# Mixture of experts in fixed slots: ranked groups, weights kept for two blocks, and a half block with stacked parts

## The reference, cut to what matters

```python
g_sel = jnp.argmax(g_logits, axis=-1)                      # one of 4 groups for each token
e_logits = jnp.take_along_axis(e_logits, g_sel[:, None, None], axis=1)[:, 0]
top_p, top_i = lax.top_k(e_prob, 2)                        # two of its 4 experts
combine = jnp.sum(one_hot(g_sel[:, None] * 4 + top_i, 16) * (g_w * top_p)[..., None], axis=1)
hid = silu(einsum('nd,edf->nef', hf, w_gate)) * einsum('nd,edf->nef', hf, w_up)   # f = 256
hid = hid * combine[..., None]
out = einsum('nef,efd->nd', hid, w_down)
```

## Time and profile before

| | |
|---|---|
| median of 3 runs | 1088.68 us |
| profiled execution: span | 1090.1 us |
| TensorE, matmul | 1073.4 us busy, 98% of the span |
| VectorE | 726.9 us, 67% |
| ScalarE | 617.3 us, 57% |
| GpSimd | 68.2 us, 6% |
| mean granted TensorE clock | 0.996 |
| read from HBM | 215.44 MB |

### The profile page before, as it was taken

One profiled execution on the slowest core, in us unless ns is written; L12 is line 12 of the kernel. 1 busy time (PEld: TensorE's weight loads), 2 busy tenths in 40 slices (PEclk: granted clock), 3 DMA queues, 4 the chain that ended last, 5 costly groups with the idle time before them and its releaser, 6 DMA issues.

```text
span 1090.1 us, 17127 instructions
## 1 busy us (share of the span) xinstructions
PE 1073.4 (98%) x7044; PEld 959.7 (88%) x7044; DVE 726.9 (67%) x815; ACT 617.3 (57%) x731; POOL 68.2 (6%) x53
## 2 busy tenths in 40 slices
PE   9999999999999999999999999999999999999997
PEld 7998889999989999998898768799999978878875
DVE  6954665865765454454875649985454778999974
ACT  7653369664465444444673537864544458877763
POOL 0600100000000000000000000000000002000332
PEclk9999999999999999999999999999999999999999
DMA  8552254654745555555346433353456467999973
GB/s 311 195 192 72 85 193 155 224 201 156 251 157 199 201 191 185 195 193 186 128 167 212 150 116 116 117 176 133 132 191 225 167 243 263 367 382 376 351 290 116
DMA packets 31922, 216.94 MB, mean 199 GB/s; under 512 B 4304, under 2 KB 4560, under 8 KB 6384
## 3 DMA queue, kind: packets, MB, share of 16 engines
q1 hardware_dynamic: 28096, 199.35, 51.5%
q0 software_dynamic: 3344, 15.24, 3.7%
q10 hardware_dynamic: 416, 1.40, 0.3%
HBM read 215.44 MB, written 3.67 MB: 201 GB/s over the span
## 4 chain that ended last, share of the span: by engine, by line
PE 89%; DVE 6%; DMA 2%; ACT 1%; issue 1%; POOL 0%; POOLq 0%; DVEq 0%; ACTq 0%
PE bank L564 27%; PE bank L566 26%; PE bank L565 26%; DVE wlo L1639 2%; PE bank L625 2%; DVE last_lo L1639 1%; DMA buf<-weights_dram,index 1%; PE bank L616 1%; PE bank L1036 1%; ACT last_hi L1122 1%; DMA raw<-weights_dram,index 1%; PE bank L958 1%; PE bank L940 1%; PE bank L706 1%; PE bank L703 1%
## 5 line engine op out<-in xcount | busy, mean ns | idle before, releaser
L1642 DVE TENSOR_TENSOR wlo<-raw,whi 128x2048 fp32r<-128x2048 f32 x138 | 317.7, 2307 | 169.2 <-ACT whi L1122 168.8
L1122 ACT ACTIVATE whi<-raw 128x2048 fp32r<-128x2048 f32 (+1 forms) x168 | 319.4, 1906 | 137.8 <-PE bank L566 134.5
L564 PE MATMUL bank<-normedT_hi,whi 128*128 128x256 f32 x640 | 177.6, 278 | 0.0
L565 PE MATMUL bank<-normedT_lo,whi 128*128 128x256 f32 x640 | 177.0, 277 | 0.0
L566 PE MATMUL bank<-normedT_hi,wlo 128*128 128x256 f32 x640 | 177.0, 277 | 0.0
L1122 ACT ACTIVATE buf<-bank 128x512 f32<-128x512 f32 (+5 forms) x147 | 70.9, 526 | 156.7 <-PE bank L566 127.9
L564 PE MATMUL bank<-xT_hi,whi 128*128 128x256 f32 (+1 forms) x448 | 127.1, 284 | 0.8 <-issue 0.8
L566 PE MATMUL bank<-xT_hi,wlo 128*128 128x256 f32 (+1 forms) x448 | 126.4, 282 | 0.0
L565 PE MATMUL bank<-xT_lo,whi 128*128 128x256 f32 (+1 forms) x448 | 126.4, 282 | 0.0
L564 PEld LDWEIGHTS bank<-normedT_hi,whi 128*128 128x128 f32 x640 | 120.1, 188 | 1.0 <-issue 0.6
L565 PEld LDWEIGHTS bank<-normedT_lo,whi 128*128 128x128 f32 x640 | 120.3, 188 | 0.7 <-issue 0.2
(11 more groups left out here) (399 smaller groups left out, 2248.4 us busy)
## 6 DMA issues: line engine op xcount, KB each, us to landing
raw<-weights_dram SPq DMA_DIRECT2D x168, 1024.0 KB, 5.0
buf<-weights_dram SPq DMA_DIRECT2D x19, 1024.0 KB, 7.0
buf<-x_dram SPq DMA_DIRECT2D x2, 512.0 KB, 4.3
buf<-mem_dram ACTq DMA_DIRECT2D x1, 1024.0 KB, 8.9
token_rows<-buf SPq DMA_DIRECT2D x1, 1024.0 KB, 8.7
buf<-final_w_dram POOLq DMA_DIRECT2D x1, 512.0 KB, 4.1
con<-consts_dram SPq DMA_DIRECT2D x1, 486.0 KB, 8.9
buf<-small_w_dram SPq DMA_DIRECT2D x1, 432.0 KB, 11.5
```

The lines of the kernel that those rows point to most:

```text
L564: E.matmul(out_, lh, rh, start=start, stop=False)
L565: E.matmul(out_, lh, rl, start=False, stop=False)
L1122: return S.activation(out_, in_, func, **kw)
L1642: V.tensor_tensor(wlo[:, n % SLOTS, :], raw[:, n % SLOTS, :], whi[:, n % SLOTS, :].bitcast(f32), sub).then_inc(piece_split, 1)
```

## The change

The number of passes stays 20, and which work is in them changes:

- The group sizes are counted first (`tot`), ranked on VectorE, and the rank decides a token's block. The fullest group has blocks 0 and 1 (256 slots), the next has block 2, the third block 3, and the smallest, which has 64 tokens at most, a half block of 64 slots (`SMALL`).
- Passes 0 to 7 are the four experts of the fullest group, each over both blocks in turn: a piece is loaded and split once and used twice. So 48 pieces are loaded in place of 60. SyncE reads the order of the groups from SBUF into a register (`value_load`) and loads all pieces by that; GpSimd loads none. No piece of an expert can be loaded before the ranks are known. The first piece is loaded, cast and split in two halves.
- Passes 12 to 15 are the smallest group. Its 64 high and 64 low columns stand side by side as one 128-wide stationary operand. One matmul with the high weights gives high x high in rows 0 to 63 and low x high in rows 64 to 127; a second one with 64 columns of the high part and the low weights is added to rows 0 to 63. That is 16 matmuls up and 8 down, where a full pass has 24 and 12. The two halves of the rows are then folded: ScalarE copies rows 64 to 127 to SBUF, VectorE adds rows 0 to 63, ScalarE's silu follows.
- The order is one list, `STEPS`. Up to pass 12 it is as before; for p over 12 the transposes of p-1 stand between the first and the second half of up(p), and down(p-1) follows right after the second half.
- A piece is fed in the step in which its slot comes free (`FED`): after first(8), for instance, none, after down(7) three at once, from pass 9 on one after each of first, second and down.

```diff
+HALF = P // 2
+SMALL = GROUPS
+TAKEN = SMALL * P + HALF
+DEEP = 12
+def expert_of(p):
+    return p // 2 if p < 8 else p - 4
+def block_of(p):
+    return p % 2 if p < 8 else (2, SMALL, 3)[p // 4 - 2]
+for _p in range(PASSES):
+    STEPS.append(("first", _p))
+    if _p > DEEP:
+        STEPS.append(("turn", _p - 1))
+    STEPS.append(("second", _p))
+    if _p:
+        STEPS.append(("down", _p - 1))
+    if _p < DEEP:
+        STEPS.append(("turn", _p))
+STEPS += [("turn", PASSES - 1), ("down", PASSES - 1)]
+FED, _last = {}, 0
+for _u in range(SLOTS, len(USES)):
+    _last = max(_last, ALL_GATHERED if _u == FOURTH else FREED[freed_by(_u)])
+    FED[_last] = _u
...
 @block.sync
+            sp.wait_ge(squares, squares_ahead["z"] + 2 * RT)
+            sp.dma_start(token_rows..., X).then_inc(rows_stored, 16)
+            sp.wait_ge(indexed, 1)
+            for u, (kind, e) in enumerate(USES):
+                if kind == 0 and e % 4 == 0:
+                    group_at[e // 4] = sp.value_load(ORDER[0:1, RANK[e // 4]:RANK[e // 4] + 1], ...)
+                if u >= RAWS:
+                    sp.wait_ge(piece_split, M0 + u + 1 - RAWS)
+                ...
+                if u == 0:
+                    sp.dma_start(RAW[raw_of(u)][:, 0:PW // 2], piece_[:, 0:PW // 2]).then_inc(first_loaded, 16)
+                    sp.dma_start(RAW[raw_of(u)][:, PW // 2:], piece_[:, PW // 2:]).then_inc(piece_loaded[raw_of(u)], 16)
+                else:
+                    sp.dma_start(RAW[raw_of(u)], piece_).then_inc(piece_loaded[raw_of(u)], 16)
...
 @block.tensor
+                    pair_, high_ = XG[0][:, 4 * half + k, at:at + P], XG[0][:, 4 * half + k, at:at + HALF]
+                    if not ends:
+                        E.matmul(b[:, :], pair_, w[0][:, k, :], start=begins, stop=False, ...)
+                    last = E.matmul(b[0:HALF, :], high_, w[1][:, k, :], start=False, stop=False, ...)
...
-            expert_up(0)
-            spread_slots()
-            gather_rest(0, 2)
-            expert_turn(0)
-            for p in range(1, PASSES):
-                expert_up(p)
-                if p <= 3:
-                    gather_rest(2 * p, 2 * p + 2)
-                expert_down(p - 1)
-                expert_turn(p)
-            expert_down(PASSES - 1)
+            gather_rest(0, 3)
+            for step, p in STEPS:
+                if step == "first":
+                    expert_up(p, 0)
+                    if p == 0:
+                        gather_rest(3, 5)
+                        spread_slots()
+                elif step == "second":
+                    expert_up(p, 1)
+                    if p == 1:
+                        gather_rest(5, 7)
+                    if p == 2:
+                        gather_rest(7, 8)
+                elif step == "turn":
+                    expert_turn(p)
+                else:
+                    expert_down(p)
...
 @block.scalar
+                if stacked(p):
+                    A(FOLD, b[HALF:P, :], ACT.Copy).then_inc(fold_copied, 1)
+                    act.wait_ge(fold_summed, expert_of(p) % 4 + 1)
+                    b, n = FOLD, HALF
+                A(SLM[0:n, :], b[0:n, 0:256], ACT.Silu, ...).then_inc(moe_silu, 1)
...
+            for i, (step, p) in enumerate(STEPS):
+                if step == "second":
+                    expert_silu(p)
...
+                elif step == "turn":
+                    act.wait_ge(moe_turned, p + 1)
+                    ... A(<high part of the hidden rows>, ...).then_inc(high["moe"], 1)
+                elif step == "down" and p == 15:
+                    fold_sums()
+                if i in FED:
+                    feed(act, M0 + FED[i])
...
 @block.vector
-            feed(dve, M0)
...
-            second_split(1).then_inc(piece_split, 1)
...
+            release(V.scalar_tensor_tensor(sizes_, bank("tot")[:, 0:GROUPS], float(GROUPS), slot_const("tie"), mult, add), "tot")
+            chain(V.tensor_tensor(bigger, ..., ALU.is_gt))
+            chain(V.tensor_reduce(ranked, bigger, AX.X, add))
+            V.scalar_tensor_tensor(block_at, ranked, 1.0, ranked, amin, add)
+            chain(V.tensor_tensor(of_rank, ..., ALU.is_equal))
...
+            V.tensor_reduce(ORDER[:, 0:GROUPS], of_rank, AX.X, amax).then_inc(indexed, 1)
...
+            for i, (step, p) in enumerate(STEPS):
+                if step == "second":
+                    expert_hidden(p)
...
+                elif step == "turn":
+                    hidden_low(p)
+                elif step == "down" and p in (6, 7, 11, 15, 19):
+                    own_added(block_of(p), p)
+                if i in FED:
+                    feed(dve, M0 + FED[i])
```

More of the change, by code:

```diff
@@ L41, with stacked @@
 SLOTTED = BLOCKS * P
+HALF = P // 2
+SMALL = GROUPS
+TAKEN = SMALL * P + HALF
 SHARED = 12
 M0 = PB["moe"]
[L44 to L48, removed]
+DEEP = 12
[3 more added lines that the diff above has]
+    return p % 2 if p < 8 else (2, SMALL, 3)[p // 4 - 2]
+def stacked(p):
+    return block_of(p) == SMALL
+STEPS = []
+for _p in range(PASSES):
[8 more added lines that the diff above has]
+STEPS += [("turn", PASSES - 1), ("down", PASSES - 1)]
+KIND = {"first": 0, "second": 1, "down": 2}
+RANK = (0, 1, 3, 2)
+USES, AT, USED_AT, FREED = [], {}, {}, {}
+for _i, (_step, _p) in enumerate(STEPS):
+    if _step == "turn":
+        continue
+    _use = (KIND[_step], expert_of(_p))
+    if _use not in AT:
+        AT[_use] = len(USES)
+        USES.append(_use)
+    if _p >= 8 or _p % 2:
+        USED_AT[AT[_use]] = M0 + len(USED_AT) + 1
+        FREED[AT[_use]] = _i
 NU = M0 + len(USES)
@@ L57, in raw_laps, with freed_by @@
     s = raw_of(u)
-    late = USES[u][1] >= EXPERTS
-    return sum(n % SLOTS == s for n in range(M0 * (not late))) + sum(raw_of(v) == s and (USES[v][1] >= EXPERTS) == late for v in range(u + 1))
-FOURTH = AT[1, 4]
+    return sum(n % SLOTS == s for n in range(M0)) + sum(raw_of(v) == s for v in range(u + 1))
+FOURTH = 6
+ALL_GATHERED = STEPS.index(("down", 1))
 def split_of(u):
     return (M0 + u) % SLOTS if u < FOURTH else SLOTS if u == FOURTH else split_of(u - 4)
+def freed_by(u):
+    return u - SLOTS if u < FOURTH else u - 4
+FED, _last = {}, 0
+for _u in range(SLOTS, len(USES)):
+    _last = max(_last, ALL_GATHERED if _u == FOURTH else FREED[freed_by(_u)])
+    FED[_last] = _u
 BANKS = {}
@@ L2240, in _ @@
+            chain(V.tensor_tensor(own, own, group, mult))
+            chain(V.tensor_reduce(slot, own, AX.X, add))
             iota = slot_const("iota")
-            for r in range(RT):
-                last = V.tensor_scalar(PICK[:, r, 0:2 * P], iota[:, 0:2 * P], extra[:, r:r + 1], own[:, r, 0:1], sub, ALU.is_equal)
-            last.then_inc(slotted, 1)
-            chain(V.tensor_tensor(slot, own[:, :, 0], extra, add))
-            for r in range(RT):
-                last = V.tensor_scalar(PICK[:, r, 2 * P:], iota[:, 2 * P:], slot[:, r:r + 1], None, ALU.is_equal)
@@ L2247, in _ @@
-            last.then_inc(slotted, 1)
+            for at, n in ((0, 2 * P), (2 * P, SLOTTED - 2 * P)):
+                for r in range(RT):
+                    last = V.tensor_scalar(PICK[:, r, at:at + n], iota[:, at:at + n], slot[:, r:r + 1], None, ALU.is_equal)
+                last.then_inc(slotted, 1)
             V.tensor_tensor(gsh, gl, bc(gmx, 4), sub).then_inc(route_max, 1)
```

336 lines of the change are left out of this document (192 added, 144 removed).

## The result

The changed kernel took 1109.49 us in the median of four runs (1107.93 to 1111.35), the kernel before 1089.61 us in four. The ratio is 1.0178, with a 95% interval of 1.0155 to 1.0201: **slower by 1.8%**, 19.9 us between the two medians. The forecast was 1105 us, range 1090 to 1116. The profiled execution has a span of 1105.8 us; the span of a run of it lies about 2.1 us under its time (1107.93 to 1105.8).

A forecast was written before the change was run, and what follows sets the result against it. TensorE was taken to set the pace, with VectorE and DMA nearly level. 8.1 + 0.5 + 6.7 + 1.6 = 16.9 us on a span of 1090.1 gave 1107.0, less 1.4 for the median: 1105.6, taken as 1105 us, range 1090 to 1116.

The forecast's parts named there:

- Start: Up to the first turn: VectorE's list of work, with the load hidden beside it, makes turn 0 8.1 us late.
- Turn 0 to 11: From turn 0 to turn 11: same steps, three gathers and two waits behind bunched feeds, 0.5 us more.
- The bunch fed after down(7): Ahead of down(8): three pieces fed together delay the low part on VectorE, a wait of 3.7 us.
- the smaller one: Ahead of down(2): two pieces fed after down(1) delay the low part on VectorE, a wait of 1.3 us.
- Turn 11 to 19: From turn 11 to turn 19: the new step order and stacked passes take 80.7 us, 6.7 us more.
- the clock: TensorE's matmuls run at 1.2 GHz after long waits; counted as 1.6 us in all.
- The walk: Step-by-step timing of the engines' queues from the end of first(12) to turn 19, giving 80.7 us from turn 11.
- two limits: From pass 13 on: step order makes a full pass 10.5 us, VectorE's work and waits a stacked one 10.0.
- The tail: The stretch after turn 19: claimed to stay as it was.
- A: Rival: TensorE keeps the pace, with low parts ready 3.0 us after first(p); median 1075 us, 1.3% faster; chance 0.15.
- B: Rival, no change: ScalarE and VectorE waits in stacked passes overlap better, start costs 2 us less; 1098 us; chance 0.17.
- C: Rival: clock falls after each wait of about 2 us, passes 16 to 18 and once in the start; 1112 us; chance 0.15.

The follow-up runs named there:

- e4: Changed kernel with SyncE loading pieces in the fixed order of groups, without waiting for the ranking or reading a register: ratio 1.0175 to the kernel before.
- e8: e3 with VectorE's work at the start reordered and the bunched feeds after down(1) and down(7) spread: 1089.4 us, ratio 0.9992 to the kernel before.
- e7: Changed kernel with TensorE running matmuls on zeros in its waits ahead of down(12) to down(17): ratio 1.0149 to the kernel before.
- e2: Changed kernel without the stack (smallest group in a full block, no fold), new order of steps kept: ratio 1.0161 to the kernel before.
- e1: Changed kernel with the stack kept, but the turn after the previous pass's down in all passes, as before: ratio 1.0120 to the kernel before.
- e5: Changed kernel with cast and split of the piece first(p) frees moved behind the low part, from pass 13 on: ratio 1.0124 to the kernel before.
- e6: e5 with that split, in stacked passes, put between the fold's addition and the hidden product: ratio 1.0048 to the kernel before.
- e9: Changed kernel with e8's start, old order of turn and down, and stacked passes among the pairs sharing weights: 1092.19 us, ratio 1.0019 to the kernel before.
- e11: e9 with cast and split of the piece a stacked pass's first half frees queued behind its hidden product: 1093.57 us, ratio 1.0032 to the kernel before.
- e12: e11 with the fourth stacked pass put behind the first expert of block 2: 1093.32 us, ratio 1.0027 to the kernel before.
- e3: Changed kernel with neither the stack nor the new order of steps: ratio 1.0033 to the kernel before.

## Why the prediction was right

**Start, +8.1; measured +8.15.** Two errors of about 1 us cancel, so that the sum fits so well is luck. The ranking cost 0.3 us and not my 1.1: the low parts began 5.12 us after the marker before and 5.38 after. And the list behind them took 13.9 us, not 12.9, 1.1 of which were short waits for casts (0.49 and 0.62). The load lies beside it, as e4 shows: the register read and the issue together took about 1 us (892.43 to 893.40), inside my 0 to 2.62; the first half landed 5.05 us after its issue, where I had 4.3.

**Turn 0 to 11, +0.5; measured +0.73.** The bunch fed after down(7) cost 12.17 - 8.41 = 3.76 us, predicted 3.7, and e8 took 3.4 of it away. It came in two parts, where I had one: TensorE waited 1.43 us ahead of second(9), for a piece of the bunch, and 1.76 ahead of down(8). For the smaller one, ahead of down(2), I had 1.3; TensorE waited 1.32 us there for the low part.

**Turn 11 to 19, +6.7, and the clock, +1.6; measured +8.26 together.** The walk's times from the end of first(12), at 1015.7, stand beside the trace: down(12) 16.5, measured 16.1; down(13) 26.5 and 26.6; down(14) 36.5 and 36.9; down(15) 46.5 and 47.8; down(16) 56.8 and 58.4; turn 19 78.6 and 80.2. What the walk lacks is the clock. With TensorE kept busy (e7) the stretch took 79.8 us, where the walk without the clock has 80.7. So the clock was mis-sized, 2.5 us for 1.6, and the walk was 0.9 too long; that they cancel to 0.0 is luck. The reason given, two limits at 10.5 and 10.0 us a pass, is shown: e2 has a period of 10.5 to 10.6 in its passes from turn 14 on, e1 of 9.86 in its stacked ones, e5 and e6 remove them one by one. It holds for the downs, of which 12 to 17 stand 10.4 to 10.9 us apart. The turns, for which I had given 10 to 10.5 us, stand 9.4 to 13.8 us apart from turn 12 to 18, and the last two 5.71, since only second(19) and down(18) lie between them. The waits of down(12) and down(16) that the profile puts down to a split are waits for the low part behind it, as said above.

**The sum.** The span came out at 1105.8, forecast 1107.0. The tail took 0.6 more, which I had put at nothing, and the passes began 2.0 us early by scatter. The median of the runs is 4.5 us over the forecast. I set the median 1.4 us under the span; but a run's time lies 2.1 us above its span, and the profiled execution of after was the fastest of its four, 1.6 us under their median.

**The rivals.** A (TensorE keeps pace, 1075 us) needs a low part 3.0 us after first(p); in after down(12) to down(17) began 4.8 to 8.4 us behind their turns. B (1098) stood on overlap between the engines; e6 shows what that overlap would have been worth, but only with another order. C (the clock falls after each wait of about 2 us in passes 16 to 18) did not come in passes 16 to 18: it fell ahead of them, at the first three downs, and once in the start (granted clock 0.85 from 895 to 905 us), behind VectorE's list. The Trainium skill, "TensorE: Matmul & The Clock Gate", section HAM oscillation, tells of a kernel with DMA waits of 3 to 5 us in which every group after a wait started at the low clock. The trace agrees for the first three downs, two of them after shorter waits (2.74 and 2.72 us), and not for the later ones, one of them after 2.79 us. Its rule that tiling doesn't speed up the way out of PSUM ("Trainium Kernel Development and Optimization", section Best Practices) points the right way: with the stack VectorE has the addition of the fold (0.67 us) on top, and TensorE's gain was lost whole in e1, e9, e11 and e12. But most of the work that binds here is the splits of weights, not PSUM.

## What to carry to other kernels

Where two engines run nearly level, work taken from one can be worth nothing until the other's order of instructions is redone: here 10.9 us less of matmuls became 7.2 us more (e1 against e3), and 1.9 more with the order partly redone (e6). Count for each pass the bare work of every engine (7.8 us of VectorE against 5.7 of TensorE tells that a stacked pass in a row can save at most 0.6 of a full pass's 8.4, not 2.7), and then walk the queue for long instructions ahead of short ones that somebody waits for: a 2.3 us split ahead of a 0.3 us low part set the period. An edit that pulls one short step ahead of the splits only hands the delay to the next short step.

## What the runs showed of the hardware

- An addition on 64 partitions of 512 columns took 0.67 us on VectorE, on 128 partitions 0.64 (1.27 for two): half the rows save nothing. The copy of such a fold on ScalarE took 0.59.
- A matmul of 128 rows by 64 columns of weights with 512 moving columns took as long as one with 128: the stack saves time by the number of matmuls alone. These are the stacked up products of e11 on TensorE's timeline, each 0.23 us behind the one before:

```profile
940.98 0.39 PE L1190 MATMUL bank<-last_hi,gathered_hi 128*128 128x512 f32 x1
941.20 0.40 PE L1191 MATMUL bank<-last_lo,gathered_hi 128*64 128x512 f32 x1
```

- The same length of wait left TensorE at either clock: 2.72 us was followed by 1.2 GHz, 2.79 by 2.4 GHz. In the 10.3 us ahead of the first TensorE was busy for 7.60 us, partly at the low clock, and in the 10.5 ahead of the second for 7.80. What decides between them the runs don't tell.
